# A mixture-of-experts kernel: the first job's down weights are issued behind its gate and up weights, ahead of the wait for the job table

## The reference

```python
gates = p_grp * jax.nn.softmax(top_logit, axis=-1)
experts = grp[:, None] * EXPERTS_PER_GROUP + top_local
...
def expert_block(args):
    xb, e = args
    return (jax.nn.silu(xb @ w_gate[e]) * (xb @ w_up[e])) @ w_down[e]
```

## Time and profile before

| | |
|---|---|
| median of 3 runs | 1967.24 us (1966.76 to 1969.73) |
| the profiled execution's own time | 1969.18 us |
| its span | 1967.4 us, mean granted clock 0.988 |
| TensorE busy | 1844.4 us, 94% |
| VectorE / ScalarE busy | 863.5 us, 44% / 764.6 us, 39% |
| moved by the DMA engines | 549.01 MB, mean 279 GB/s |
| chain of waits, by engine | PE 51%, DMA 37%, DVE 7% |

### The profile page before, as it was taken

One profiled execution on the slowest core, in us unless ns is written; L12 is line 12 of the kernel. 1 busy time (PEld: TensorE's weight loads), 2 busy tenths in 40 slices (PEclk: granted clock), 3 DMA queues, 4 the chain that ended last, 5 costly groups with the idle time before them and its releaser, 6 DMA issues.

```text
span 1967.4 us, 29089 instructions
## 1 busy us (share of the span) xinstructions
PE 1844.4 (94%) x10231; PEld 1163.7 (59%) x10231; DVE 863.5 (44%) x1647; ACT 764.6 (39%) x1394; POOL 77.4 (4%) x98
## 2 busy tenths in 40 slices
PE   8999999988999999999999999998999999999997
PEld 6779998875799988863333333335975333333333
DVE  5766656669765567861111111114883111111113
ACT  5554334547543345423333333334532333333333
POOL 3300000120000000100000000000010000000000
PEclk9999999988999999999999999999999999999999
DMA  9645565541355546229999999997508999999995
GB/s 316 202 138 194 192 193 171 160 151 33 117 193 193 190 145 192 95 111 404 422 422 422 422 422 422 422 422 270 192 22 332 422 422 422 422 422 422 422 422 205
DMA packets 154612, 549.01 MB, mean 279 GB/s; under 512 B 10702, under 2 KB 70440, under 8 KB 106152
## 3 DMA queue, kind: packets, MB, share of 16 engines
q1 hardware_dynamic: 151128, 539.52, 71.0%
q0 software_dynamic: 3088, 8.10, 1.4%
q10 hardware_dynamic: 320, 0.34, 0.1%
HBM read 546.81 MB, written 1.11 MB: 279 GB/s over the span
## 4 chain that ended last, share of the span: by engine, by line
PE 51%; DMA 37%; DVE 7%; ACT 2%; issue 2%; POOL 1%; SPq 0%; ACTq 0%; POOLq 0%; DVEq 0%
DMA raw<-in_w_expert_down 36%; PE pb L1166 26%; PE pb L1722 6%; PE pb L1461 6%; PE pb L1691 3%; PE pb L1295 1%; PE pb L1272 1%; PE pb L1395 1%; PE pb L1318 1%; DVE parts L1855 1%; PE pb L1658 1%; POOL rms L726 1%; PE pb L1178 1%; DMA raw<-in_w_in 1%; ACT parts L746 1%
## 5 line engine op out<-in xcount | busy, mean ns | idle before, releaser
L1691 PE MATMUL pb<-raw,xw 128*64 128x512 f32 x2016 | 486.4, 606 | 1.3
L1855 DVE TENSOR_TENSOR parts<-raw,parts 128x2048 fp32r<-128x2048 f32 (+1 forms) x138 | 307.3, 2232 | 121.6 <-ACT parts L746 118.5
L2445 DVE TENSOR_TENSOR qk<-qk,pb 128x256 f32<-128x256 f32 x126 | 52.9, 421 | 666.9 <-ACT qk L1035 666.9
L746 ACT ACTIVATE parts<-raw 128x2048 fp32r<-128x2048 f32 (+1 forms) x138 | 256.6, 1867 | 221.2 <-PE pb L1166 162.4
L1166 PE MATMUL pb<-xT,parts 128*128 128x256 f32 (+1 forms) x2712 | 333.3, 283 | 0.0
L1166 PEld LDWEIGHTS pb<-xT,parts 128*128 128x128 f32 (+1 forms) x2712 | 329.2, 191 | 4.7 <-issue 2.9
L1722 PE MATMUL pb<-raw,qk 128*64 128x512 f32 x1008 | 242.5, 602 | 63.6 <-DMA raw<-in_w_expert_down 60.9
L1166 PE MATMUL pb<-parts,xT 128*128 128x512 f32 (+1 forms) x1200 | 272.6, 386 | 1.8 <-DVE parts L1855 1.3
L1691 PEld LDWEIGHTS pb<-raw,xw 128*64 128x64 f32 x2016 | 123.7, 136 | 227.3 <-issue 162.7
L1166 PEld LDWEIGHTS pb<-parts,xT 128*128 128x128 f32 x1200 | 218.3, 189 | 48.0 <-issue 4.3
L1722 PEld LDWEIGHTS pb<-raw,qk 128*64 128x64 f32 x1008 | 67.0, 136 | 236.7 <-issue 160.9
(11 more groups left out here) (316 smaller groups left out, 1391.1 us busy)
## 6 DMA issues: line engine op xcount, KB each, us to landing
raw<-in_w_expert_gate SPq DMA_DIRECT2D x126, 1024.0 KB, 12.7
raw<-in_w_expert_up SPq DMA_DIRECT2D x126, 1024.0 KB, 12.4
raw<-in_w_expert_down SPq DMA_DIRECT2D x126, 1024.0 KB, 12.7
raw<-in_w_ffn_gate SPq DMA_DIRECT2D x22, 1024.0 KB, 5.4
raw<-in_w_ffn_up SPq DMA_DIRECT2D x22, 1024.0 KB, 5.3
raw<-in_w_ffn_down SPq DMA_DIRECT2D x22, 1024.0 KB, 5.0
raw<-in_w_in SPq DMA_DIRECT2D x16, 1024.0 KB, 6.1
raw<-in_w_in_ab SPq DMA_DIRECT2D x11, 1024.0 KB, 12.5
```

The costliest lines, as they stand in the source:

```text
L746: nc.scalar.activation(parts[:, (SPL0[seg] + k) % SPL, 0, 0:kk * nn], raw[:, place, 0:kk * nn], ACT.Copy).then_inc(hi_done[seg], 1)
L1691: ins = mm(pb[m][rows, :], xw[:, 4 * hf + k, :], w[:, k, :], start=(hf == 0 and k < 2), stop=(hf == 1 and k >= 2))
L1855: v.tensor_tensor(two[:, 1, :], raw[:, place, 0:kk * nn], two[:, 0, :].bitcast(F32), ALU.subtract)\
L2445: v.tensor_tensor(d, d, pb[2 + m][:].rearrange("p (k i s) -> p k i s", k=4, i=2)[:, :, 1, :], ALU.add)\
```

## The change

Down loads of job 0 are issued directly behind its gate and up loads, with the constant 0 for the expert, and ahead of SP's wait for the table. `step(1)` (the only call with a Python integer) then ends after the gate and up loads of job 1. In the loop, the number of the expert for the down loads is read behind the gate and up loads and no longer ahead of them. `load_job` itself is as it was: the places and the counts that are waited for are the same.

```diff
                 for q, m, hf in gate_up(0):
                     load_job(l, 0, 0, q, m, hf)
+                for hf in range(2):
+                    load_job(l, 1, 0, down_at(False) + hf, 2, hf)
                 sp.wait_ge(tab_done, l + 1)
                 more = sp.value_load(tab[0:1, 2 * JOBS:2 * JOBS + 1], min_val=NS // W - 2, max_val=JOBS - 2)
 
                 def step(j):
-                    e, e1 = expert(at(j, 1, 0)), expert(at(j, 1, -1))
+                    e = expert(at(j, 1, 0))
                     for q, m, hf in gate_up(j):
                         load_job(l, j, e, q, m, hf)
+                    if isinstance(j, int):
+                        return
+                    e1 = expert(at(j, 1, -1))
                     for hf in range(2):
                         load_job(l, j, e1, down_at(False) + hf, 2, hf)
```

## The result

| | before | changed |
|---|---|---|
| median | 1968.18 us (4 runs, 1966.76 to 1969.73) | 1982.16 us (4 runs, 1980.91 to 1983.88) |
| ratio | | 1.0071, 95% interval 1.0059 to 1.0083 |
| span of the profiled run | 1967.4 us | 1982.1 us |

The change makes the kernel 14.0 us slower, 0.7%. The forecast was +12.3 us and 1979.5 us; the measured time lies in its range, 1975.5 to 1986 us. It is 2.7 us above the forecast: 1.7 us are the change's, and 0.9 us come from a fourth run of the kernel before, which moved its median from 1967.24 to 1968.18 us.

The account below looks back on a forecast made before the run. Transfers at 422 GB/s were taken to bound both expert loops. Per layer, 6.83 us lost less old holes plus 1.9 us new gave 5.8 and 6.5 us, +12.3 on 1967.24: 1979.5 us, range 1975.5 to 1986.

Parts of the forecast that it names:

- SyncE's order: Loop start: first down load at 878.3, half a microsecond earlier; job 1's gate loads move from 865.21 to about 882.
- What the stream loses: Loads moved before 878.3 (layer 1) or 1490.5 (layer 2) no longer move: 2.88 MB, 6.83 us a layer.
- What comes back: Behind the release, old holes of 2.97 and 2.27 us are filled, less 1.9 us of new holes a layer.
- TensorE's first jobs: At job 1, TensorE waits about 4 us for gates but frees places in time for job 2's first gate load: hidden.
- Rival A: Half clock for all of job 1 frees places 3.1 us late, 6.2 us in both layers: 1985.7 us; chance 0.13.
- The bound of 13.7 us: Upper end of the slowdown, both layers together, if new holes equal the old 2.97 and 2.27 us.
- In the loop: Reading the down expert's number behind the up loads, at most 0.7 us, is hidden by the queue: zero cost.
- B (no change): Gate loads at the loop starts were hidden anyway: 1967.2 us; chance 0.03.
- C (faster): In the loop, gate loads issued up to 0.7 us earlier shorten the job; at 0.3 us, 1960.6 us; chance 0.03.
- D (less than 10.8 us): Early down weights leave no hole but the start: about 9.5 us slower, 1976.7 us; chance 0.06.
- The rate of 358 GB/s: Skill page's HBM limit: each 2.88 MB would cost 8.0 us, not 6.8, slowdown some 2.4 us larger; trace preferred.
- fell once before: Under rival A: TensorE's clock fell once, to 0.51 from 884 to 886, after tiny products; a product took 3.31 us.

Follow-up runs that it names:

- wait_only: The kernel before with one added SyncE wait for a count of 4 in `used` ahead of the table reads, load order untouched: 1989.20 us, ratio 1.0101.
- free_places: The changed kernel with job 0's down weights in the ring's two free places, job 1's gate loads waiting for TensorE instead: 1968.29 us, ratio 0.9993 to the kernel before.
- between: The kernel before with job 0's down loads put behind job 1's gate loads and ahead of its up loads: 1971.58 us, ratio 1.0016.
- second_only: The changed kernel with job 0's down loads early in the second layer only: 1975.71 us, ratio 1.0038 to the kernel before.
- again: The changed kernel, unedited, timed once more: 1983.26 us, ratio 1.0069 to the kernel before.
- spin: The changed kernel with nine idle products on TensorE in its new wait for job 1's gate weights: 1981.30 us, ratio 1.0055 to the kernel before.
- loop_read: The kernel before with only the down expert's number read behind the gate and up loads: 1969.47 us, ratio 1.0003.

## Why the prediction was right, and where it was short

- **SyncE's order.** The down loads go 5.41 us behind TensorE's start (878.77 and 873.36; 1498.07 and 1492.66), 0.5 us earlier than the 5.93 us of before, as said. The gate loads follow at 882.39; that the table reads cost nothing is not shown apart from the stream's slow start. `wait_only` and `free_places` show that it is this wait in front of table-bound loads, and nothing about down before gate, that costs.
- **What the stream loses.** 2.88 MB a layer, 6.83 us, was the main term. The windows show it gone (1 and 0 GB/s), and `between` and `second_only` go with it.
- **What comes back.** This term was mis-sized. I took 1.9 us of new holes a layer. From the landings they are 7.47 - 6.83 + 2.97 = 3.6 us and 7.01 - 6.83 + 2.27 = 2.5 us (3.3 and 2.3 us with the landings of `again`). The windows of the changed kernel, counted from the first down load's issue, give less, 3.1 and 2.1 us: from layer 1's 92/422 of 11.55 and 11/422 of 39.15 us, 3.5 us together, goes the 0.46 us by which this loop began later, and layer 2 lacks 18/422 of 48.6 us. Of the 1.9 us the start alone was to be 1.2 us, and it took 2.0 and 1.8 us (windows above). The row that I took it from said more: I went by the DMA share of 0.85 from 866 to 868, and by the 242 GB/s of the same row the stream lacks 1.6 us between the issue at 865.21 and 868.
- **TensorE's first jobs: "Hidden."** This is the step that failed, in the first layer and by 1.0 to 1.3 us. I worked out the margin for job 2's first gate load only (free at 891.3 at half clock, needed by 893.2). Even that margin was too wide: job 1's first gate half was used from 889.25 and not from 888.0, its product took 3.68 and not 3.31 us, and the load was issued at 893.11, only 0.6 us ahead of its need (878.77 + 6 x 2.485 = 893.7). The second one, which stands behind the slow product, a turn and the next product, was issued at 896.45 (893.11 + 3.67 - 0.33). Counted from the first down load's issue it was needed by 878.77 + 7 x 2.485 = 896.2, and from 898 to 902 the stream shows the hole of 1.1 us. By my count the load was late by 0.3 us only, so the count explains where the hole is, not all of its size; that it hangs on the clock is what `spin` shows. Rival A had this mechanism, with a half clock over all of job 1 and 3.1 us in both layers; it lasted for the first product and the turn behind it, and `spin` puts it at 1.0 to 1.3 us in layer 1 and at nothing in layer 2.
- **The bound of 13.7 us** was therefore none. "The old holes, nothing gained" is no upper end when the change makes a new wait that opens new holes. The measured +14.0 is just outside it, by less than the play of the times; the hole of 1.1 us (0.5 in `again`) from 898 to 902 has no place in the bound.
- **What stays open**: how the 2 us of the start divide between the transfers' own beginning and the two loads that were alone in the queue until 882.39; I ran nothing that takes this apart. Open too are the 0.4 to 0.5 us a layer between landings and windows, and why half the clock cost nothing in the second layer.
- **In the loop.** Zero, confirmed by `loop_read` and by 422 GB/s in both. Rivals B (no change) and C (faster) fell; D (less than 10.8 us) too.
- **The rate of 358 GB/s.** With the 358 GB/s of the Trainium skill, "DMA: Bandwidth & Descriptors", section "Bandwidth", the slowdown would be about 14.7 us, an estimate from the page. It is near the measured size by luck: both kernels move 422 GB/s in the loop. The section itself gives 358 GB/s as a core's share when both cores of a pair stream, and this kernel runs on one.

## What to carry to other kernels

In a loop that a stream of loads paces, what a change at its start is worth is the bytes that it moves, or no longer moves, ahead of the consumer's release of a buffer, and the holes that it opens or closes behind it: a queue that runs in order must not put a load that waits for a buffer ahead of loads whose buffers are free. Here moving a load earlier brought nothing while the number of buffers stayed the same, and room that is idle in just this stage, used for the first few steps, brought 19 us. When the change makes a new wait, follow the buffers behind it one by one with the slow clock, and not only the first.

## What the runs showed that I had not expected

TensorE's granted clock fell to half (0.50, 1.2 GHz) in its wait of 5.10 us and was still there for the work behind it: the product at 889.25 took 3.68 us, and the window from 894 to 896 is the first to rise (0.81). Windows of the changed kernel:

```profile
890.00:892.00 2.00, 2.00 (x8) 0.47 (x4) 0.00 (x0) 0.00 (x0) 0.00 (x0) 0.50 0.97 410
892.00:894.00 2.00, 2.00 (x10) 0.81 (x8) 0.00 (x0) 0.00 (x0) 0.00 (x0) 0.50 1.06 446
894.00:896.00 2.00, 2.00 (x8) 0.64 (x10) 1.18 (x3) 0.69 (x2) 0.00 (x0) 0.81 0.96 406
```

In the first layer the wait need not be what made it fall. The kernel before, without such a wait, fell at the same place, behind the stretch of products with one column (0.51 from 884 to 886), and so did `spin` (0.50), whose TensorE had idle products in place of the wait; both were back at 1.00 from 888 on, the changed kernel only from 896 on. With the wait the half clock lasted longer. In the second layer the kernel before stayed at 1.00, where the same instructions ran, and the changed kernel fell behind the start of its wait (0.94 from 1504 to 1506, then 0.50). The waits of 0.63 us in each job of the loop left it at 1.00. The prediction's "fell once before" overlooks its own row of 864 to 866, at 0.50: the clock was half there too, shortly ahead of the loop.
